# Dilated attention heads: value products as plain float32 matmuls on unsplit operands

## The reference

```python
s = jnp.einsum('brnqhd,brnkhd->brnhqk', qf, kf).astype(jnp.float32) / math.sqrt(dh) + bias
s = jnp.where(valid[:, None], s, -jnp.inf)
m = jnp.max(s, axis=-1, keepdims=True)
p = jnp.exp(s - m)
den = jnp.sum(p, axis=-1)
o = jnp.einsum('brnhqk,brnkhd->brnqhd', p.astype(v.dtype), vf).astype(jnp.float32)
```

## Time and profile before

| | us |
|---|---|
| median of 3 runs | 1701.59 |
| lowest, highest run | 1696.47, 1703.51 |
| span of the profiled execution | 1704.9 |
| PE busy | 1652.8 (97%) |
| PE weight loads | 1396.6 (82%) |
| DVE busy | 1166.5 (68%) |
| ACT busy | 800.6 (47%) |
| POOL busy | 365.0 (21%) |

### The profile page before, as it was taken

One profiled execution on the slowest core, in us unless ns is written; L12 is line 12 of the kernel. 1 busy time (PEld: TensorE's weight loads), 2 busy tenths in 40 slices (PEclk: granted clock), 3 DMA queues, 4 the chain that ended last, 5 costly groups with the idle time before them and its releaser, 6 DMA issues.

```text
span 1704.9 us, 27622 instructions
## 1 busy us (share of the span) xinstructions
PE 1652.8 (97%) x9138; PEld 1396.6 (82%) x9138; DVE 1166.5 (68%) x2301; ACT 800.6 (47%) x1997; POOL 365.0 (21%) x228
## 2 busy tenths in 40 slices
PE   6999999999999999999999999999999999999998
PEld 4777888888888888888878787877999998987886
DVE  5631123322328888888888888887788678878897
ACT  5531113211215555555555555556898788862000
POOL 2203000000000000000000000002477667772232
PEclk9999999999999999999999999999999789999999
DMA  5337756699769555755665556432777767646441
GB/s 188 133 127 263 288 216 242 207 281 288 247 207 267 173 166 185 239 160 162 192 228 161 161 159 210 155 123 86 215 204 220 206 202 207 213 157 227 142 167 74
DMA packets 217988, 330.36 MB, mean 194 GB/s; under 512 B 52414, under 2 KB 142201, under 8 KB 211517
## 3 DMA queue, kind: packets, MB, share of 16 engines
q1 hardware_dynamic: 213372, 319.26, 59.1%
q0 software_dynamic: 2400, 9.48, 1.7%
q10 hardware_dynamic: 2080, 0.01, 0.1%
HBM read 203.00 MB, written 121.34 MB: 190 GB/s over the span
## 4 chain that ended last, share of the span: by engine, by line
PE 82%; DVE 5%; DMA 3%; issue 3%; ACT 3%; SPq 2%; POOL 1%; DVEq 0%; ACTq 0%; POOLq 0%
PE proj L413 24%; PE proj_a L1116 14%; PE out_ps L1969 7%; PE wt_ps L1080 7%; PE o_ps L1099 4%; PE o_ps L1101 4%; PE z_ps L1070 3%; PE z_ps L1069 3%; PE pt_ps L1492 3%; PE oa_ps L1512 3%; PE oa_ps L1511 2%; PE s_ps L1483 2%; PE s_ps L1484 2%; ACT prob L1546 1%; SPq L1400 1%
## 5 line engine op out<-in xcount | busy, mean ns | idle before, releaser
L1150 ACT ACTIVATE WT_hi<-wt_ps 128x512 fp32r<-128x512 f32 (+1 forms) x320 | 171.0, 534 | 316.6 <-PE wt_ps L1080 316.6
L1197 DVE TENSOR_TENSOR_SCAN W<-w,W,zeros 128x512 f32<-128x512 f32 x192 | 248.3, 1293 | 58.9 <-ACT w L1142 58.2
L413 PE MATMUL proj<-h_hi,w_hi 128*128 128x512 f32 x608 | 247.2, 407 | 4.7 <-DVE h_lo L598 3.5
L413 PE MATMUL proj<-h_lo,w_hi 128*128 128x512 f32 x608 | 241.3, 397 | 0.0
L413 PE MATMUL proj<-h_hi,w_lo 128*128 128x512 f32 x608 | 241.1, 397 | 0.0
L1205 DVE TENSOR_TENSOR WT_lo<-wt_ps,WT_hi 128x512 fp32r<-128x512 f32 (+1 forms) x320 | 187.4, 586 | 2.2 <-ACT WT_hi L1150 2.2
L1080 PE MATMUL wt_ps<-ident,W 128*128 128x128 f32 x1088 | 173.4, 275 | 6.5 <-DVE WT_lo L1205 5.7
L1546 ACT ACTIVATE prob<-neg_s,rows 128x256 f32<-128x256 f32 (+1 forms) x384 | 173.5, 454 | 11.5 <-DVE rows L1601 10.1
L1051 POOL TENSOR_TENSOR y_sum<-y_sum,gate 64x512 f32<-64x512 f32 x32 | 41.2, 1287 | 627.2 <-DVE y_sum L1212 627.2
L1142 ACT ACTIVATE w<-z_ps 128x512 f32<-128x512 f32 (+2 forms) x320 | 169.2, 529 | 8.1 <-PE z_ps L1070 8.1
L1080 PEld LDWEIGHTS wt_ps<-ident,W 128*128 128x128 f32 x1088 | 131.7, 140 | 42.5 <-DVE WT_lo L1205 15.2
(11 more groups left out here) (206 smaller groups left out, 3534.7 us busy)
## 6 DMA issues: line engine op xcount, KB each, us to landing
va_d<-st SPq DMA_DIRECT2D x96, 256.0 KB, 3.7
wa_hi<-wa_d SPq DMA_DIRECT2D x48, 512.0 KB, 3.8
wa_lo<-wa_d SPq DMA_DIRECT2D x48, 512.0 KB, 4.9
va<-va_d SPq DMA_DIRECT2D x24, 1024.0 KB, 8.7
wa_d<-x_sb SPq DMA_DIRECT2D x24, 512.0 KB, 3.8
w_raw<-in_w_tiles SPq DMA_DIRECT2D x18, 512.0 KB, 5.1
x_sb<-in_x SPq DMA_DIRECT2D x16, 512.0 KB, 5.5
qk_hi_d<-st SPq DMA_DIRECT2D x32, 256.0 KB, 2.5
```

Of the source, the lines that this page charges most:

```text
L413: last = pe.matmul(acc_of(n)[:], w[w_slot(t)][:, k, :], h[ch][:, k, :], start=(k, a) == (0, 0), stop=(k, a) == (KD - 1, 2))
L1150: act.activation(WT_hi[n % PART_SLOTS][:, cols], t_ps[n % T_SLOTS][:, cols], ACT.Copy) \
L1197: dve.tensor_tensor_scan(W[n % W_SLOTS][:, 0:width][:, ::-1], w[n % W_IN][:, 0:width][:, ::-1], above[:, ::-1], first, ALU.mult, ALU.max). ...
```

## The change

The probabilities are no longer split: DVE copies the transposed ones as they are (`copy_weights`), and a block has one matmul, of plain float32 operands, with 64 columns. The values are stored unsplit, in the 128 columns that their two halves had, for two heads together: three stores per group where there were six, and each of the three value tiles is loaded once for a pair, by SP in the even head (dilation 1) and in the odd head for the next pair (dilations 16 and 4). A bank now holds 8 tiles; there are 6 banks a head, not 12, and ACT alone takes a bank out into `rows` (`take_out`), a step after it is done; `copy_low`, `high_part`, `low_part` and `add_halves` go. The ring of transposed probabilities has 8 slots in place of 4 + 4 (the memory is the same). Scores, exponentials, transposes, merge, reordering and all lags of PE stay.

```diff
-    STORES = {"qk": 2, "gate": 1, "vb": 1, "va": 6}
+    STORES = {"qk": 2, "gate": 1, "vb": 1, "va": 3}
...
-                src = st[n % ST_SLOTS][:].rearrange("p (b h x) -> p b h x", b=QB, h=2)
-                for hh in range(2):
-                    for dst in (va_d[0][2 * j + hh, :, ch * QB:(ch + 1) * QB, :],
-                                va_d[1][2 * j + hh, :, ch, :].rearrange("(b p) x -> p b x", p=P),
-                                va_d[2][2 * j + hh, cols, :].rearrange("(b p) x -> p b x", p=P)):
-                        sp.dma_start(dst, src[:, :, hh, :]).then_inc(done, 16)
+                src = hi.rearrange("p (b x) -> p b x", b=QB)
+                for dst in (va_d[0][j, :, ch * QB:(ch + 1) * QB, :],
+                            va_d[1][j, :, ch, :].rearrange("(b p) x -> p b x", p=P),
+                            va_d[2][j, cols, :].rearrange("(b p) x -> p b x", p=P)):
+                    sp.dma_start(dst, src).then_inc(done, 16)
...
+                    if kind == "va":
+                        act.activation(st[n % ST_SLOTS][:, 0:CH // 2], vtp[v % V_SLOTS][:, 0:CH // 2], ACT.Copy) \
+                            .then_inc(first_done, 1)
+                        return
...
+                    if kind == "va":
+                        dve.tensor_copy(st[n % ST_SLOTS][:, CH // 2:CH], vtp[v % V_SLOTS][:, CH // 2:CH]) \
+                            .then_inc(second_done, 1)
+                        return
...
-    OBANKS = 3 * NTILE // 4
+    PER_BANK = CH // DH
+    OBANKS = 3 * NTILE // PER_BANK
...
-        return ORDER.index(c) * (NTILE // 4) + idx // 4
-
-
-    LAG_T, LAG_H, LAG_L, LAG_V, LAG_O = 2, 2, 2, 4, 5
+        return ORDER.index(c) * (NTILE // PER_BANK) + idx // PER_BANK
...
-    NEG_SLOTS, SCORE_SLOTS, PART_SLOTS = 2, 4, 4
+    NEG_SLOTS, SCORE_SLOTS, PART_SLOTS = 2, 4, 8
...
-        va2 = m.sb("va2", [P, TB, 2 * DH], F32R)
+        va2 = m.sb("va2", [P, TB, 2 * DH])
...
-        PT_hi = m.ring("PT_hi", PART_SLOTS, [P, CH], F32R)
-        PT_lo = m.ring("PT_lo", PART_SLOTS, [P, CH], F32R)
+        PT = m.ring("PT", PART_SLOTS, [P, CH])
...
+            def load_values(pair, c):
...
-                sp.dma_start(v[c][:].bitcast(F32), src.rearrange("p (n x) -> p n x", x=2 * DH)).then_inc(v_loaded[c], 16)
+                sp.dma_start(v[c][:], src.rearrange("p (n x) -> p n x", x=2 * DH)).then_inc(v_loaded[c], 16)
...
-                if not start:
-                    sp.wait_ge(pv_done, PART_SLOTS + at(it, STEPS, par * NB))
-                    load_values(at(it, 2, par), 0)
+                if par == 0 and not start:
+                    sp.wait_ge(pv_done, PART_SLOTS + at(it, STEPS, 0))
+                    load_values(it, 0)
                 rows_of(it, par, 2)
-                if not last:
-                    load_values(after_head, 2)
+                if par == 1 and not last:
+                    load_values(at(it, 1, 1), 2)
                 move_second(it, par)
...
                 move_first(it, par)
-                if not last:
-                    load_values(after_head, 1)
+                if par == 1 and not last:
+                    load_values(at(it, 1, 1), 1)
...
-                pe.wait_ge(lo_done, 2 + at(it, STEPS, b + 1))
+                pe.wait_ge(copy_done, 2 + at(it, STEPS, b + 1))
                 for c, idx, r, n, nk, col in bunch:
                     bank = par * OBANKS + bank_of(c, idx)
-                    if idx == 0:
-                        pe.wait_ge(v_loaded[c], at(it, 32 * V_LOADS[c], 16 * V_LOADS[c] * (par + 1)))
-                    if idx % 4 == 0:
+                    if idx == 0 and par == 0:
+                        pe.wait_ge(v_loaded[c], at(it, 16, 16))
+                    if idx % PER_BANK == 0:
 
                         pe.wait_ge(rows_done, at(it, 2 * OBANKS, bank + 1))
-                    out = o_ps[bank % 2][:, (idx % 4) * P:(idx % 4 + 1) * P]
+                    place = idx % PER_BANK
+                    out = o_ps[bank % 2][:, place * DH:(place + 1) * DH]
                     for kb in range(nk):
                         w = slice(col + kb * P, col + (kb + 1) * P)
-                        vk = v[c][:, idx - nk + 1 + kb, :]
-                        pe.matmul(out, PT_hi[b % PART_SLOTS][:, w], vk, start=(kb == 0), stop=False)
-                        last = pe.matmul(out, PT_lo[b % PART_SLOTS][:, w], vk, start=False, stop=(kb == nk - 1))
+                        last = pe.matmul(out, PT[b % PART_SLOTS][:, w], v[c][:, idx - nk + 1 + kb, par * DH:(par + 1) * DH],
+                                         start=(kb == 0), stop=(kb == nk - 1))
...
-            def high_part(it, b):
-                width = BUNCHES[b % NB][1]
-                act.wait_ge(pt_done, SCORE_SLOTS + at(it, STEPS, b + 1))
-                act.wait_ge(pv_done, at(it, STEPS, b + 1))
-                act.activation(PT_hi[b % PART_SLOTS][:, 0:width], t_ps[b % 2][:, 0:width], ACT.Copy).then_inc(hi_done, 1)
-
-            def copy_low(it, par, bank, b):
+            def take_out(it, par, bank, b):
 
                 n = par * OBANKS + bank
                 act.wait_ge(pv_done, PART_SLOTS + at(it, STEPS, b + 1))
-                act.wait_ge(rows_done, at(it, 2 * OBANKS, n + 1))
-                src = o_ps[n % 2][:].rearrange("p (i a d) -> p i a d", i=4, a=2)
-                act.activation(o_low[n % 2][:], src[:, :, 1, :], ACT.Copy).then_inc(low_copied, 1)
+                c, part = ORDER[bank // (NTILE // PER_BANK)], bank % (NTILE // PER_BANK)
+                act.activation(rows[par][:, c, PER_BANK * part:PER_BANK * (part + 1), 0:DH],
+                               o_ps[n % 2][:].rearrange("p (i d) -> p i d", d=DH), ACT.Copy).then_inc(rows_done, 1)
...
-                        copy_low(turn, b // NB, bank, b)
-                if then := behind(it, before, s, STEPS, LAG_H):
-                    high_part(*then)
+                        take_out(turn, b // NB, bank, b)
...
-            def low_part(it, b):
+            def copy_weights(it, b):
                 width = BUNCHES[b % NB][1]
-                dve.wait_ge(hi_done, at(it, STEPS, b + 1))
+                dve.wait_ge(pt_done, SCORE_SLOTS + at(it, STEPS, b + 1))
                 dve.wait_ge(pv_done, at(it, STEPS, b + 1))
-                dve.tensor_tensor(PT_lo[b % PART_SLOTS][:, 0:width], t_ps[b % 2][:, 0:width],
-                                  PT_hi[b % PART_SLOTS][:, 0:width].bitcast(F32), ALU.subtract).then_inc(lo_done, 1)
-
-            def add_halves(it, par, bank, b):
-                n = par * OBANKS + bank
-                dve.wait_ge(low_copied, 2 + at(it, 2 * OBANKS, n + 1))
-                src = o_ps[n % 2][:].rearrange("p (i a d) -> p i a d", i=4, a=2)
-                c, quad = ORDER[bank // 4], bank % 4
-                dve.tensor_tensor(rows[par][:, c, 4 * quad:4 * quad + 4, 0:DH], src[:, :, 0, :],
-                                  o_low[n % 2][:], ALU.add).then_inc(rows_done, 1)
+                dve.tensor_copy(PT[b % PART_SLOTS][:, 0:width], t_ps[b % 2][:, 0:width]).then_inc(copy_done, 1)
...
-                if then := behind(it, before, s, STEPS, LAG_O):
-                    turn, b = then
-                    for bank in BANKS_AFTER[b % NB]:
-                        add_halves(turn, b // NB, bank, b)
-                if then := behind(it, before, s, STEPS, LAG_L):
-                    low_part(*then)
+                if then := behind(it, before, s, STEPS, LAG_C):
+                    copy_weights(*then)
...
+    va_d = [nc.dram_tensor("va1_d", [HEADS // 2, P, TB, 2 * DH], F32),
+            nc.dram_tensor("va4_d", [HEADS // 2, CH, NCH, 2 * DH], F32),
+            nc.dram_tensor("va16_d", [HEADS // 2, T, 2 * DH], F32)]
```

25 lines of the change are left out of this document (10 added, 15 removed).

## The result

The changed kernel takes 1674.53 us (median of 4 runs, 1673.66 to 1676.31), the kernel before 1700.05 us beside it (1696.47 to 1703.51): a ratio of 0.9847 [0.9823, 0.9871], 25.5 us less. The forecast was 1668 with a range of 1648 to 1694 and 0.82 for faster. The number holds. The mechanism behind it does not.

A forecast was written before the change was run, and what follows sets the result against it. PE bounded the kernel before, and POOL's loop was to bound the dilated phase after. Start -6.5, six periods -22.6 and end -4.7 gave -33.8: 1671 us of span, 1668 against the median, range 1648 to 1694.

The forecast's parts named there:

- Records of a plain product: Value products on PE: a plain float32 product gives two records, a load and a product, so 1200 records remain.
- 1200 x (111 - 57) = 65 us less PE work: Value products in the dilated phase: plain loads start 57 ns apart instead of 111, saving PE 8.1 us per head.
- Rival 1: Plain loads on PE are as long as rounded ones, PE keeps 36 us a head; -24, 1678 us, chance 0.32.
- POOL's loop: Merge, reorderings and the way back to the merge bound the dilated heads: 37.3 us per odd period.
- The start and the end: Before head 1's step 4, -6.5 us; from head 7's step 4 to the output products, -4.7 us.
- Both lie under POOL's loop and cost nothing: ACT falls from 35.5 to at most 26 us a head, DVE from 33.4 to 28.3, both claimed hidden.
- Values and SP's queue: 24 value loads of 1 MB become 12; PE's 1.46 us wait and the half clock after it go.
- Rival 2: SP's queue becomes the loop, POOL still waits 3.55 us for the next head's q; 1679 us, chance 0.10.
- Half clock: PE standing still before each head's step 4 costs 3.4 us of lost clock per gap, a 7 us stretch.
- Rival 3: Long half clock follows each gap before a head's step 4, PE loses 11.7 us per head; 1712 us, chance 0.11.
- The sum: Whole kernel: -6.5 start, -22.6 six periods, -4.7 end make -33.8 on the 1704.9 us span, so 1671.
- From span to median: The profiled span before was 3.3 us above the median of 1701.6, so 1671 became 1668 us.

The follow-up runs named there:

- (9): Changed kernel, but ACT first copies transposed probabilities to a tile nobody reads, DVE's copy waits for it, and their ring has 4 slots; 1687.00 us.
- (10): Changed kernel plus as many ACT copies, of the identity to a spare tile, waiting for nothing of PE's, with a probability ring of 4 slots; 1676.52 us.
- experiment 1: Changed kernel plus 14 groups of 16 equal products before the dilated phase, only their records read; plain 128 x 64 loads start 0.112 us apart.
- experiment 2: Changed kernel, but a pair's three value tiles are loaded again for the odd head, 24 loads of 1 MB; 1695.14 us, 0.9961 of before.
- experiment 4: Changed kernel with probabilities and values rounded and one rounded product per block, 600 value product records instead of 1200, lower accuracy; 1671.55 us.

## Why the prediction was right, and where it was wrong

| kernel | us | step |
|---|---|---|
| before | 1700.1 | |
| 12 loads, adds kept | 1694.6 | -5.5 |
| 12 loads, no adds | 1692.4 | -2.2 |
| plain products, ACT then DVE (9) | 1687.0 | -5.4 |
| the same ACT work, no wait (10) | 1676.5 | -10.5 |
| the change | 1674.5 | -2.0 |

The rows are medians from different groups of runs, beside which the kernel before took 1698.7 to 1700.1. The -2.2 is not clear of noise, and what the -5.4 comes of (plain products, six banks in place of twelve, DVE's copy in place of its subtraction) was not taken apart. The steps depend on their order: each wait removed uncovers the next. The adds alone give nothing that could be told, the loads alone 5, and the loads given back at the end cost 20.6. The split was never taken out of the first kernel by itself.

- **Records of a plain product.** Two, as taken from the earlier trace rows. Right.
- **The term that failed: 1200 x (111 - 57) = 65 us less PE work.** The pitch is 111 before and after. The step was "I take the fast load, since the nearest row in columns and type lies on that line". The rows compared were lengths of records, which say nothing of the pitch: a plain load of 128 columns lasts 192 ns at a pitch of 112, one of 64 columns 138 at 58 (experiment 1). The sign that spoke against it was in the same rows: with 128 columns, a record of 192 ns already stood beside a pitch of 111, so a length was no pitch. Rival 1, at 0.32, is the case that came.
- **POOL's loop.** Its turn was put at 30.1 + 6.1 + 1.1 = 37.3; it is 30.6 + 5.6 at full clock. It stays just under PE. The 41.4 us given for the second period before were 40.4. The periods came to rival 1's, whose 36.4 and 39.9 are 36.0 to 36.4 and 38.5: its 1.3 us of waiting for the merge did not come.
- **The start and the end.** -6.5 and -4.7 forecast, -1.3 and -1.7 measured (rival 1: 0 and -1).
- **"Both lie under POOL's loop and cost nothing"**, said of the ACT and DVE work removed. This is the largest thing that was missed: 12.5 us, of which 10.5 is the hand-over from PE over ACT to DVE and 2.0 the occupation of ACT (experiments 9, 10). Busy time of 33 and 35 us under a PE of 36 was taken for cover. With the same busy time and no hand-over it is one, to 2.0 us (experiment 10).
- **Values and SP's queue.** Priced as the 1.46 us wait and the half clock after it. Both went. But the loads act mostly through the rows' trip and DVE's small sums, and are worth 20.6 us once the other waits are gone (experiment 2). Rival 2 had named this queue, as something that could stay; halving the loads is what moved it out of the way. POOL's wait of 3.55 us for q fell to 0.56.
- **Half clock.** None came behind the first S4. Rival 3 has its case in experiment 4, with 0.76 to 0.90; there the lost clock stayed within the time that PE would have waited anyway, but for one period of 39.1 us at 0.76, in which PE was busy for 38.6. What the forecast did not price by itself is the half clock that the kernel before loses: its third and fourth period, at 0.90 and 0.81, hold some 13.5 of the 27.6 us in the profiled execution. The runs hold less of it. Of the 64 runs of the kernel before that stand beside the experiments, the two with a granted clock of 0.998 took 1694.6 and 1694.9 us, the six at 0.986 or less 1707.0 to 1713.1. By these, as an estimate, some 5 of the 25.5 us are half clock and some 20 are waits.
- **The sum.** Span 1671 forecast, 1671.8 measured, by -6.5, -22.6 and -4.7 where -1.3, -27.6 and -1.7 came, and 1.2 us at the phase's beginning. These add up to 31.8; the other 1.3 came in the output phase. The agreement is chance: 65 us of work did not go, and some 30 us of waits and half clock did.
- **From span to median.** The 3.3 us were taken off, since the profiled execution before was above its median. After, the median is 2.7 above the profiled span. This makes 6 of the 6.5 us by which 1668 misses 1674.5. A run's time is 1.7 to 1.9 us above its own span (1673.69 and 1671.8), so the profiled execution before was, as an estimate, one of some 1706.7 us, well above the median.

## What to carry to other kernels

Price work on TensorE by the distance between the starts of neighbouring loads, never by the length of a record. When an operation is handed over two engines, do not cost it at nothing because each of the two has slack: look at what stands behind the waiting instruction on its queue, and whether that feeds the engine waited for. And when several small waits cover each other, removing one of them from the first version can give nothing, while giving one back in the final version shows its cost: here 0 and 5 us by taking out the adds and half of the loads, 20.6 and 12.5 by giving back the loads and ACT's copy, more together than the 25.5 of the whole change. And look at the granted clock of a burst before its pitch is read.
